# Broadcast rows fetched by DMA from a DRAM scratch in place of TensorE broadcasts, in a two-block transformer kernel

## The chip, the cores and the metric

The kernel runs on one core of a Trainium2 chip. The metric is the device time of one execution in microseconds (us). The five engines are called PE (TensorE matmul; PEld is its weight load), DVE (VectorE), ACT (ScalarE), POOL (GpSimd) and SP (SyncE, which here only issues DMAs).

## What is computed

Two blocks over 256 tokens of 1024 features, with 256 context tokens beside them, all in float32. The change is in the first block, a layer with a gated delta rule. Cut to what matters (forward direction; the backward one is the same on flipped tokens):

```python
proj = jnp.einsum('bld,dp->blp', hn, w_in)            # q,k,v | a,b | z_dn | u_pool | z_pool
qkv = jax.nn.silu(_short_conv(qkv, conv_w))
q, k = _l2_norm(q), _l2_norm(k)                       # every row to unit length
g = -jnp.exp(a_log) * jax.nn.softplus(ab[0] + dt_bias)
beta = jax.nn.sigmoid(ab[1])
# _gated_delta_rule, in chunks of 128 tokens: G = running sum of g in the chunk,
# decay factors exp(-|G_i - G_j|) between tokens, exp(G_i) on the queries
state = state * exp(G_last) + einsum('bhcd,bhcv->bhdv', k_i, v_new)
```

Behind it stand the output product, three feed-forward layers, a short-convolution mixer, a latent attention and a last feed-forward layer; the change leaves them as they are.

## The kernel before

**Layout.** Activations lie with features on the 128 partitions and the 512 tokens along the row. Every weight chunk (128 x 1024 values, eight 128 x 128 tiles) is loaded by SP into a ring of three `w_raw` buffers (L413), split by ACT into a high part `w_hi` (L777) and by POOL into a low part `w_lo` (L524), and used by PE in three products for each tile (L549, L550, L553). ACT splits chunk c+2 once chunk c-1 is done (`split_ahead`, `AHEAD = 2`).

**Order.** Each engine runs one hand-written instruction list in order; semaphores join them. In the input stage the chunks of `w_in` pass one after another: gates, keys, values, queries, then 26 tail items (`IN_TAIL`), here called n = 0 to 25. A "u" item is one of eight pooling inputs, which DVE turns into a pooled difference (`pooled_difference`); a "z" item gets a SiLU on ACT; items 13 and 25 are the pooling products themselves. ACT can write `u_hi(4)` only when item 13 is done on PE, for it reuses a buffer that item 13 reads.

**Unit lengths.** ACT takes square roots of the inverse squared lengths into `rk` (32 x 128) and `rq` (16 x 128) at n = 4 (`unit_length`, L999, L1000). The length of a token must then reach all partitions. PE does that with a one-hot stationary operand (`spread_lengths`, L894): four matmuls for each of 12 parts j (eight key heads, four pairs of query heads), placed behind the tail items n = 10, 11, 13, 14, 16, 17, 19, 20, 21, 22, 23 and 24, into bank 7 or 6, and DVE multiplies `kT` or `qT` by that bank (`scaled_by_length`, L1152).

**Running sums.** At n = 7 PE sums the gate terms and DVE copies them to `cum` (L1134 to L1139, semaphore `cum_ready`).

**The recurrence.** Eight rounds r = 0 to 7, each with a forward (FWD) and a backward (BWD) batch of four heads. `sums` (L1306) puts the running sums of a batch on all partitions, four matmuls with a broadcast gate column. `decay` on ACT turns them into `dec` = exp(-|G_i - G_j|) (four Abs at L1544, one Exp at L1548). `gram` (L1315) makes the keys' products, `masked_gram` on DVE (L1335) masks them, and `first_blocks` (DVE L1706 to L1717) starts the triangular inverse, whose matmuls are `left` (L1379) and `right` (L1390). Between two rounds PE does, for FWD and then BWD: `gram(r+1)`, `sums(r+1)`, `new_values(r)` (L1413). In rounds 4 to 7 the queries' factor exp(G) is made by ACT at the end of the round before, from the same bank as `sums` (`query_decay`, L1555), POOL multiplies it by the queries (L1682), and `out_four` (L1528, L1530) reads it. `dec` shares its room with `atl`, which `left` reads at its levels 3 and 4, and with the normalised inputs of the input stage. In between, PE works off 96 parts of the conditioning product (`mod_part`, L593), whose data SP streams through a ring of six buffers (L434).

## Time and profile before

| | |
|---|---|
| time, median of 3 runs (lowest to highest) | 2383.66 us (2382.59 to 2388.62) |
| the profiled execution: its time, its span | 2388.25 us, 2386.5 us |
| busy share of the span: PE, DVE, ACT, POOL | 96%, 38%, 33%, 43% |
| granted TensorE clock, mean | 0.981 of full |
| DMA: data moved, mean rate | 297.41 MB, 125 GB/s |

The span runs from 0 to 2386.5 us. The tail items of the input stage fill it up to about 289 us, the recurrence stands from there to about 560 us, and nothing behind that is edited. A busy engine is not necessarily the bound: the chain of waits and the timeline say which engine the next one waited for. In a timeline a bracket after a row is the idle time before it and what ended it.

### The profile page before, as it was taken

How to read it: one execution, taken by the hardware profiler on the slowest of the kernel's cores; microseconds unless marked ns; L12 is line 12 of the kernel's file. 1: busy time of each engine (PE TensorE's matmuls, PEld its weight loads, DVE VectorE, ACT ScalarE, POOL GpSimd, SP SyncE). 2: the span in 40 equal slices, each digit the busy share in tenths (PEclk: the TensorE clock that was granted, in tenths of full speed). 3: DMA queues.
4: the chain of work that ended last, by engine and by line, in shares of the span. 5: the costliest groups of instructions: out<-in, count | busy, mean ns of one | idle time of the engine just before them, and what ended most of it. 6: DMA issues, size and time to landing. Idle time of an engine off the chain costs nothing.

```text
span 2386.5 us, 37010 instructions
## 1 busy us (share of the span) xinstructions
PE 2280.5 (96%) x14398; PEld 1821.1 (76%) x14398; DVE 910.1 (38%) x1572; ACT 782.9 (33%) x1232; POOL 1024.2 (43%) x473
## 2 busy tenths in 40 slices
PE   6999999998979999999999999999999999898999
PEld 2788877776768888878877888887888887547999
DVE  4466456655551221153372131133121124756312
ACT  2445443332232222222223223224222223424444
POOL 0446522423524444434443444443444443204888
PEclk9999999999989999999999999999999999989999
DMA  7234455545625233224323423232432322203655
GB/s 253 89 101 138 151 204 187 187 150 197 223 69 170 95 97 95 90 79 150 121 92 113 142 90 98 90 96 80 168 96 91 97 94 71 71 0 91 192 184 185
DMA packets 82682, 297.41 MB, mean 125 GB/s; under 512 B 9072, under 2 KB 11504, under 8 KB 82288
## 3 DMA queue, kind: packets, MB, share of 16 engines
q1 hardware_dynamic: 82400, 295.06, 37.7%
q8 instruction: 108, 1.77, 0.3%
q10 hardware_dynamic: 144, 0.34, 0.1%
q14 instruction: 30, 0.25, 0.0%
HBM read 294.31 MB, written 1.05 MB: 124 GB/s over the span
## 4 chain that ended last, share of the span: by engine, by line
issue 57%; POOL 21%; PE 18%; DVE 2%; POOLq 1%; ACT 0%; DVEq 0%; ACTq 0%
POOL w_lo L524 21%; PE bank L549 3%; PE bank L550 3%; PE bank L553 3%; PE bank L593 2%; PE bank L1379 1%; PE bank L1390 1%; PE bank L1315 1%; PE bank L894 1%; PE bank L1362 0%; DVE gdn_outer L1727 0%; PE bank L1402 0%; PE bank L1306 0%; PE bank L1413 0%; POOLq L529 0%
## 5 line engine op out<-in xcount | busy, mean ns | idle before, releaser
L524 POOL TENSOR_TENSOR w_lo<-w_raw,w_hi 128x1024 fp32r<-128x1024 f32 x383 | 931.9, 2437 | 1159.8 <-ACT w_hi L777 1159.0
L549 PE MATMUL bank<-n_hi,w_lo 128*128 128x512 f32 (+1 forms) x2216 | 792.4, 358 | 18.0 <-ACT n_hi L748 9.3
L553 PE MATMUL bank<-n_lo,w_hi 128*128 128x512 f32 (+1 forms) x2216 | 786.2, 355 | 0.6 <-DVE n_lo L701 0.3
L550 PE MATMUL bank<-n_hi,w_hi 128*128 128x512 f32 (+1 forms) x2216 | 786.3, 355 | 0.0
L777 ACT CAST w_hi<-w_raw 128x1024 fp32r<-128x1024 f32 x383 | 401.5, 1050 | 770.5 <-PE bank L553 760.3
L549 PEld LDWEIGHTS bank<-n_hi,w_lo 128*128 128x128 f32 x2216 | 420.5, 190 | 95.4 <-issue 27.9
L553 PEld LDWEIGHTS bank<-n_lo,w_hi 128*128 128x128 f32 x2216 | 420.3, 190 | 67.0 <-DVE n_lo L701 2.5
L550 PEld LDWEIGHTS bank<-n_hi,w_hi 128*128 128x128 f32 x2216 | 420.7, 190 | 63.8
L2101 DVE TENSOR_TENSOR prod<-silu,bank 128x512 f32<-128x512 f32 (+1 forms) x88 | 54.6, 622 | 723.2 <-PE bank L553 723.1
L549 PE MATMUL bank<-g_hi,w_lo 128*128 128x512 f32 (+1 forms) x768 | 283.1, 369 | 1.4 <-DVE g_lo L2092 1.4
L550 PE MATMUL bank<-g_hi,w_hi 128*128 128x512 f32 (+1 forms) x768 | 283.1, 369 | 0.0
L553 PE MATMUL bank<-g_lo,w_hi 128*128 128x512 f32 (+1 forms) x768 | 283.0, 369 | 0.0
L2063 DVE SCALAR_TENSOR_TENSOR h<-bank,gates,h 128x256 f32<-128x256 f32 x136 | 60.7, 480 | 298.3 <-PE bank L553 298.1
L549 PEld LDWEIGHTS bank<-g_hi,w_lo 128*128 128x128 f32 x768 | 144.0, 188 | 28.8 <-DVE g_lo L2092 1.8
L553 PEld LDWEIGHTS bank<-g_lo,w_hi 128*128 128x128 f32 x768 | 144.0, 188 | 27.3
L550 PEld LDWEIGHTS bank<-g_hi,w_hi 128*128 128x128 f32 x768 | 144.0, 188 | 27.2
L2049 ACT ACTIVATE silu<-bank 128x512 f32<-128x512 f32 (+1 forms) x88 | 47.8, 544 | 284.9 <-PE bank L553 284.8
L1083 DVE SCALAR_TENSOR_TENSOR conv<-bank,cols,conv 128x508 f32<-128x508 f32 (+3 forms) x96 | 63.0, 659 | 58.8 <-ACT conv L1024 56.3
L2092 DVE TENSOR_TENSOR g_lo<-prod,g_hi 128x512 fp32r<-128x512 f32 (+1 forms) x88 | 84.6, 963 | 1.7 <-ACT g_hi L2039 1.5
L757 DVE TENSOR_TENSOR nt<-h 128x512 f32<-128x512 f32 (+1 forms) x77 | 79.1, 1028 | 2.6
L1661 POOL TENSOR_TENSOR gdn_t<-gdn_inner,consts 128x256 f32<-128x256 f32 x16 | 13.1, 817 | 155.3 <-DVE gdn_inner L1709 155.3
L593 PE MATMUL bank<-mod_raw,cond 128*32 128x512 f32 x256 | 60.1, 661 | 18.3 <-DMA mod_raw<-in_modstream 18.3
(320 smaller groups left out, 1964.6 us busy)
## 6 DMA issues: line engine op xcount, KB each, us to landing
w_raw<-in_stream SPq DMA_DIRECT2D x383, 512.0 KB, 3.5
mod_raw<-in_modstream SPq DMA_DIRECT2D x64, 512.0 KB, 5.6
late<-in_modstream SPq DMA_DIRECT2D x56, 512.0 KB, 4.6
w_raw<-in_modstream SPq DMA_DIRECT2D x48, 512.0 KB, 5.7
h<-in_tokens SPq DMA_DIRECT2D x1, 2048.0 KB, 11.6
consts<-in_consts SPq DMA_DIRECT2D x1, 1152.0 KB, 9.6
h<-in_ctx SPq DMA_DIRECT2D x1, 1024.0 KB, 8.8
out<-h SPq DMA_DIRECT2D x8, 128.0 KB, 3.6
```

The costliest lines, as they stand in the source:

```text
L524: nc.gpsimd.tensor_tensor(w_lo[:, slot, :], w_raw[:, slot, :], w_hi[:, slot, :].bitcast(F32), ALU.subtract).then_inc(w_lo_ready, 1)
L549: nc.tensor.matmul(out_ap, wl, hi, start=start, stop=False)
L550: nc.tensor.matmul(out_ap, wh, hi, start=False, stop=False)
L553: return nc.tensor.matmul(out_ap, wh, lo, start=False, stop=stop)
L593: last = nc.tensor.matmul(bank[MOD_BANK][32 * j:32 * j + 32, :], cond[:, which, k, :], room[:, jj * 512:(jj + 1) * 512], start=(k == 0), s ...
L757: square = nc.vector.tensor_tensor(nt[:, k % 2, s_], h[:, k, s_], h[:, k, s_], ALU.mult)
L777: nc.scalar.copy(w_hi[:, c % RING, :], w_raw[:, c % RING, :]).then_inc(w_hi_ready, 1)
L1083: ins = nc.vector.scalar_tensor_tensor(acc[:, :, to], src[:, :, of], col(Cols.CONV + ci * CONV + j), acc[:, :, to], ALU.mult, ALU.add)
L2049: nc.scalar.activation(silu[:, f % 2, 0:w], bank[(g0 + g) % BANKS][:, 0:w], ACT.Silu).then_inc(gate_ready, 1)
L2063: last = nc.vector.scalar_tensor_tensor(h[:, d, s_], bank[g % BANKS][:, s_], gates[:, gate, d, c:c + 1], h[:, d, s_], ALU.mult, ALU.add)
L2092: nc.vector.tensor_tensor(g_lo[:, f, 0:w], prod[:, f % 2, 0:w], g_hi[:, f, 0:w].bitcast(F32), ALU.subtract).then_inc(hid_lo, 1)
L2101: nc.vector.tensor_tensor(prod[:, f % 2, 0:w], silu[:, f % 2, 0:w], bank[g % BANKS][:, 0:w], ALU.mult).then_inc(groups_read, 2)
```

## The change

- `spread_lengths` is gone. ACT stores `rk` and `rq` to a DRAM scratch (`length_rows`) right after the square roots, and later loads each part back to all 128 partitions with a DMA whose source repeats one 2 KB row 128 times (`load_lengths`). The loads go into four rooms of `conv` and `act_out` that the convolutions have left. They are issued from ACT behind n = 7 (parts 0 to 3), 12 (4, 5), 15 (6, 7), 18 (8, 9) and 21 (10, 11). DVE multiplies from there.
- `sums` is gone. PE transposes `cum` once behind n = 10 (`turn_sums`), ACT copies it out and stores it behind n = 12 (`keep_sums`), and every batch's rows are loaded into `dec` itself (`load_decay`), two DMAs in front of round 0 and then two for each round, behind ACT's copies of level 4.
- The queries' factor gets a DMA of its own (`load_query_decay`, in rounds 4 to 7) and is made in its own round, between ACT's copies of level 2 and of `at`.
- PE's waits for `a_dec` and `a_qd` ahead of `key_rows` and ahead of the transposes of `a` are gone, since bank `b0` holds no sums any more. Some semaphores that nothing used are removed.

```diff
+    cum_rows = nc.dram_tensor("cum_rows", (64 * P,), F32).ap()
+    length_rows = nc.dram_tensor("length_rows", (6 * HEADS * P,), F32).ap()
+    def to_all(rows, first):
+        return bass.AP(rows.tensor, first * P, [[0, P], [1, 4 * P]])
...
+    KQ_LOADS = {7: (0, 1, 2, 3), 12: (4, 5), 15: (6, 7), 18: (8, 9), 21: (10, 11)}
+    def length_room(j):
+        return (conv, act_out)[j % 4 // 2][:, j % 2, :]
+    def turn_sums(pe):
+        pe.wait_ge(cum_ready, 1)
+        nc.tensor.transpose(bank[MISC_BANK][0:64, 0:P], cum[:].rearrange("p t g -> p (t g)"), C(Const.IDENT))\
+            .then_inc(gb_turned, 1)
...
-            for j in KQ_AFTER.get(n, ()):
-                spread_lengths(pe, j)
+            if n == 10:
+                turn_sums(pe)
...
-            nc.scalar.activation(rk[:], rk[:], ACT.Sqrt)
+            nc.scalar.activation(rk[:], rk[:], ACT.Sqrt).then_inc(kq_rstd, 1)
             nc.scalar.activation(rq[:], rq[:], ACT.Sqrt).then_inc(kq_rstd, 1)
+            act.wait_ge(kq_rstd, 2)
+            act.dma_start(length_rows[0:4 * HEADS * P].rearrange("(r c) -> r c", c=P), rk[:]).then_inc(rows_out, 16)
+            act.dma_start(length_rows[4 * HEADS * P:].rearrange("(r c) -> r c", c=P), rq[:]).then_inc(rows_out, 16)
+        def load_lengths(j):
+            if j == 0:
+                act.wait_ge(rows_out, 32)
+                act.wait_ge(tile_used, 24)
+            if j >= 4:
+                act.wait_ge(kq_scaled, j - 3)
+            act.dma_start(length_room(j), to_all(length_rows, 4 * j)).then_inc(length_full[j % 4], 16)
+        def keep_sums():
+            act.wait_ge(gb_turned, 2)
+            nc.scalar.copy(gb[:, 0:P], bank[MISC_BANK][0:64, 0:P]).then_inc(ab_act, 1)
+            act.wait_ge(ab_act, 5)
+            act.dma_start(cum_rows.rearrange("(r c) -> r c", c=P), gb[:, 0:P]).then_inc(rows_out, 16)
...
-            nc.vector.tensor_tensor(dest, dest, bank[kq_bank(j)][:], ALU.mult).then_inc(kq_scaled, 1)
+            nc.vector.tensor_tensor(dest, dest, length_room(j), ALU.mult).then_inc(kq_scaled, 1)
...
-                    sums(pe, r + 1, d)
...
-            act.wait_ge(g_cb, n + 1)
-            if r:
-                act.wait_ge(g_p1, nth(6, r - 1, 3, d))
+            act.wait_ge(rows_in[d], 16 * (r + 1))
             for j in range(4):
-                last = nc.scalar.activation(w["dec"][:, j], b4(b0)[:, j], ACT.Abs,
+                last = nc.scalar.activation(w["dec"][:, j], w["dec"][:, j], ACT.Abs,
...
+        act.wait_ge(rows_out, 48)
+        for d in (FWD, BWD):
+            load_decay(0, d)
         for d in (FWD, BWD):
             decay(0, d)
...
             tail_copy(r, 1, FWD)
+            if with_x:
+                load_query_decay(r)
...
+            if with_x:
+                query_decay(r)
             for n, d, t, hs, b0, gc in batches:
                 act.wait_ge(g_at, n + 1)
...
                     tail_copy(r, li, d)
+                    if li == 4 and r + 1 < len(ROUNDS):
+                        load_decay(r + 1, d)
```

## Rows read from the trace of the kernel before

**Rows 1.** Windows: stretch, length, busy us (count) of each engine, granted clock, DMA share, GB/s

```profile
263.00:274.00 11.00, 11.00 (x88) 10.37 (x88) 4.77 (x8) 4.15 (x7) 7.19 (x4) 1.00 0.48 143
357.00:389.00 32.00, 30.77 (x511) 23.40 (x511) 20.88 (x50) 12.86 (x35) 8.17 (x8) 1.00 0.55 197
```

**Rows 2.** Chain of work that ended last, the length broadcasts: start, us, what

```profile
229.90 1.08 PE bank L894 x8
233.97 1.08 PE bank L894 x8
240.90 1.08 PE bank L894 x8
...
283.28 1.08 PE bank L894 x8
```

**Rows 3.** Timeline of ACT in the input stage: start, us, instruction, [idle before]

```profile
212.28 0.29 ACT L1000 ACTIVATE rq<-rq 16x128 f32<-16x128 f32 x1
...
221.62 1.05 ACT L777 CAST w_hi<-w_raw 128x1024 fp32r<-128x1024 f32 x1
...
241.01 0.40 ACT L994 CAST u_hi<-boxr 128x256 fp32r<-128x256 f32 x1 [5.68 <-PE bank L553]
```

**Rows 4.** Timeline of POOL in the input stage

```profile
242.71 7.17 POOL L524 TENSOR_TENSOR w_lo<-w_raw,w_hi 128x1024 fp32r<-128x1024 f32 x3 [4.90 <-ACT w_hi L777]
```

**Rows 5.** Timeline of DVE in the input stage

```profile
228.79 0.23 DVE L1139 TENSOR_TENSOR e_tail<-tot,cum 128x64 f32<-128x64 f32 x1
```

**Rows 6.** Timeline of PE: three idle times

```profile
204.31 0.60 PE L860 MATMUL bank<-decay_rate,consts 16*128 16x16 f32 x2 [3.50 <-DVE decay_rate L1117]
...
224.05 0.35 PE L549 MATMUL bank<-n_hi,w_lo 128*128 128x256 f32 x1 [1.39 <-POOL w_lo L524]
...
461.56 0.46 PE L1528 MATMUL bank<-gdn_qdec,state 128*128 128x128 f32 x2 [1.77 <-DVE gdn_rhs L1761]
```

**Rows 7.** Windows, behind the first of these idle times

```profile
206.00:208.00 2.00, 2.00 (x12) 2.00 (x11) 0.00 (x0) 0.00 (x0) 2.00 (x1) 0.50 0.51 199
```

**Rows 8.** DMA issues: line, queue, count, KB each, median us to landing; one ACT issue

```profile
mod_raw<-in_modstream SPq DMA_DIRECT2D x64, 512.0 KB, 5.6
rope<-in_rope ACTq DMA_DIRECT2D x1, 331.0 KB, 3.1
...
L2352 ACTq DMA_DIRECT2D rope<-in_rope x1: 379/379/379, 2024.0 to 2024.0; - x1
```

**Rows 9.** Chain of work that ended last, from round 1 to round 2

```profile
353.29 0.89 PE bank L1306 x8
...
355.08 0.91 PE bank L1315 x8
358.69 0.96 DVE gdn_inner L1712
359.70 0.68 PE bank L1379 x16
```

**Rows 10.** Timeline of DVE and of PE, from round 6 to round 7

```profile
539.99 0.95 DVE L1712 TENSOR_TENSOR gdn_inner<-gdn_inner,consts 128x256 f32<-128x256 f32 x1
...
545.12 0.68 PE L1379 MATMUL bank<-gdn_outer,gdn_inner 64*64 64x64 f32 x16
```

**Rows 11.** Timeline of ACT: a level-4 copy of round 1; `decay` of round 0, FWD

```profile
341.09 0.37 ACT L1560 COPY gdn_t<-bank 128x256 f32<-128x256 f32 x1 [1.52 <-PE bank L1379]
...
289.42 1.14 ACT L1544 ACTIVATE gdn_dec<-bank,neg_cum 128x128 f32<-128x128 f32 x4 [4.78 <-PE bank L553]
...
291.87 0.63 ACT L1548 ACTIVATE gdn_dec<-gdn_dec 128x512 f32<-128x512 f32 x1
```

**Rows 12.** Waits of SP in the recurrence: us in total, times, longest us

```profile
SPq L434 <- PE bank L593: 205.3, 37, 18.3
```

**Rows 13.** DVE's square of two SBUF inputs: beside an idle POOL; the mean of all (page, costliest groups)

```profile
15.00 0.69 DVE L757 TENSOR_TENSOR nt<-h 128x512 f32<-128x512 f32 x1
...
L757 DVE TENSOR_TENSOR nt<-h 128x512 f32<-128x512 f32 (+1 forms) x77 | 79.1, 1028 | 2.6
```

68 lines of the change are left out of this document (22 added, 46 removed).

## The prediction, made before the changed kernel ran

> **What bounds the kernel now.** I read the windows by stage first. Look at PE's busy time against the length of the stretch: in the tail of the input stage it is busy 11.00 of 11.00 us, in a round of the recurrence 30.77 of 32, both at full clock [rows 1]. So PE time taken out there shows in the end time, until another engine's chain becomes the longer one. The chain of waits then says which PE work stands on the path: all 12 length broadcasts do [rows 2], and so does the FWD broadcast of sums between two rounds [rows 9]. The timelines of ACT, POOL and DVE say how soon another engine takes over. Behind the recurrence everything hangs on its end (SP loads the next chunks only then), so what is saved ahead of it is saved in the whole.
>
> **Input stage, what is removed.** From one broadcast to the next it is 4.07 us with one chunk between them and 6.93 with two [rows 2]. So a chunk takes 2.86 and a broadcast 1.21 us, twelve of them 14.5. The transpose that comes in is one matmul of the four in a broadcast: 0.3.
>
> **Input stage, what ACT takes on.** A DMA issue holds ACT for 0.38 us; between issue and landing a 331 KB load took 3.1 us and the 512 KB loads of the modulation stream 5.6 [rows 8]. The new ones carry 256 KB. I walk through the items with these numbers.
>
> At n = 4 two issues and the wait for the roots put about 0.9 us behind 212.28 [rows 3]. The next pooling input starts that much later, and the chain runs through DVE, ACT and POOL to the idle time of 1.39 us in which PE waits for `w_lo` at 224.05 [rows 6]; PE passes the 0.9 us on in full. At n = 7 four issues (1.5 us, of which the running SiLU hides 0.3) stand ahead of the cast at 221.62 [rows 3] and of the fourth pooling input. So `cum_ready`, at 229.0 [rows 5], comes at 229.0 + 0.9 + 1.2 = 231.1. Item 10 ends at 229.9 + 0.9 = 230.8, the transpose waits until 231.1, and item 11 starts at 231.5, where it started at 229.90 + 1.08 = 231.0. So far 0.5 us is lost.
>
> Items 11, 12 and 13 then take 3 x 2.86, and item 13 ends at 240.1 (before: 240.9 [rows 2]). Here is the next obstacle. ACT may write `u_hi(4)` only now (241.01, after 5.68 us idle [rows 3]); behind it stand the SiLU and the cast of chunk 15, and POOL works from 242.71, 7.17 us for three chunks [rows 4]. The low part of chunk 15 was therefore ready at 245.1, 4.2 us after item 13. Two broadcasts and chunk 14 covered this with 5.3 us; now chunk 14 alone covers 2.86. In addition `keep_sums` stands ahead of that cast (copy and wait, about 0.4 us) with three issues (1.15): ready at 240.1 + 4.2 + 1.5 = 245.8. PE idles 2.8 us and starts chunk 15 at 245.8, before 240.9 + 2 x 1.21 + 2.86 = 246.2. The gain up to here is 0.4 us, and four broadcasts have gone.
>
> From there seven more broadcasts (j = 4 to 10) go until 283.28, and PE is the bound: a chunk's cast (1.05 [rows 3]) and low part (2.4) with SiLU and two issues are done 5.1 us after the chunk that frees them, where PE needs them after 2 x 2.86 = 5.7. That is 7 x 1.21 = 8.5. The loads at n = 15, 18 and 21 wait for products that DVE makes only behind a pooled difference; three times 0 to 0.5 us, I take 0.5 in all. Item 24 ends 0.4 + 8.5 - 0.5 = 8.4 us earlier. Bounds: 13.0 if ACT's issues cost PE nothing and nothing stalls (11 x 1.21 - 0.3); 3 if each wait costs a microsecond more and the clock falls once.
>
> DVE's product now reads two SBUF tiles beside a working POOL. A square of two such inputs takes 0.69 us alone and 1.03 in the mean [rows 13]. For two products per part pair that is 0.7 us, in DVE time that is idle, so I cost it at nothing; if the cover is gone, it is in the 0.5 above. The Trainium skill ("SBUF — State Buffer", section "Who interferes with whom") says that a DVE instruction with two SBUF inputs and a GpSimd instruction that reads SBUF exclude each other for whole instructions. By that rule a product could wait for a whole low part; the gain would then be some 3 us less.
>
> **First round.** The twelfth broadcast began at 283.28 and the FWD Exp of `decay` ended at 292.50, 9.2 us later, with 3.1 us from its first Abs on [rows 2, 11]. Now ACT issues the two loads about 0.8 us after item 24. SP has just sent the context tokens and three modulation parts, so I take 3.5 us to landing (bounds 2.5 and 6). `dec` is there 0.8 + 3.5 + 3.1 = 7.4 us after item 24, 1.8 earlier; with a little for the second issue I take 1.5 (bounds: a landing in 3.1 us gives 2.2, one in 5.6 a loss of 0.3). The page "DMA: Bandwidth & Descriptors" of the Trainium skill (section on the anatomy of one DMA) gives about 2 us plus the bytes at 436 GB/s, an estimate of 2.6 us here, by which this term would be 2.4.
>
> **Between the rounds.** The chain runs `gram` FWD, `sums` FWD (0.89), `new_values` FWD, `gram` BWD (355.08), then DVE until 359.65, and `left` at 359.70 [rows 9]. Without `sums` FWD, `gram` BWD ends 0.89 us earlier, and DVE, which waits for it, too. `sums` BWD stands beside DVE's chain and is worth nothing. In front of round 7, DVE is done at 540.94 and `left` starts at 545.12 [rows 10]: PE itself is the bound there, and both broadcasts count, 1.78. Together 6 x 0.89 + 1.78 = 7.1 us (bounds: 6.2 if DVE holds the last one too, 8.9 if PE itself bounds two more).
>
> **What hides the new work of the rounds.** `load_decay` is issued behind the level-4 copy at 341.09 [rows 11]. `first_blocks` wants `dec` once `gram` BWD (then over at 355.1) is masked (0.7), and `decay` takes 1.8 (3.1 less the 1.3 of a table load between its Abs and its Exp [rows 11]); so the rows must be there by 354, 12 us after their issue, against 3.1 to 5.6. The issues (0.38) stand in waits for PE such as the 1.52 us there. The queries' two Exp (0.63 each) fall into ACT's wait for the transposes of `a`; with that cover gone they cost 1.3 us in each of four rounds. SP waited 205.3 us for PE in the recurrence [rows 12], so DMA time is to be had for 0.5 to 1 MB more a round. PE no longer waits for `a_dec` and `a_qd`, and it did not before.
>
> **Sum.** 8.4 + 1.5 + 7.1 = 17.0 us. The profiled execution took 2388.25 us (a span of 2386.5), so 2371.2 of its own kind. The median of the runs, 2383.66, is 4.6 us lower: 2366.7.
>
> **Rivals.**
> *Nothing takes over from PE.* If ACT's sequencer issues the DMAs beside its running work and the cast of chunk 15 is in time, it is 13.0 + 2.2 + 8.9 = 24 us: 2360. For it: ACT is busy 4.15 of 11 us [rows 1]. Against it: its idle time is waiting for PE, and the issues come behind that wait. Chance 0.2.
> *The clock falls.* After idle times of 1.39 and 1.77 us PE stays at 2.4 GHz; after 3.50 it runs on at a granted clock of 0.50, 1.2 GHz [rows 6, 7]. The change makes idle times of 2.8 at chunk 15, of 2.3 at 224 and of about 2.7 (1.77 + 2 x 0.89 - 0.89) in front of rounds 5 and 6, all between. Each fall costs about one chunk's time, 2.9 us; three of them leave 8 us: 2375. Chance 0.17.
> *The input stage gives nothing.* The chain of ACT, DVE and POOL is longer than walked, and only the rounds gain, 6 us: 2378, no change that could be told. Chance 0.1.
> *Slower: the rows land late.* All 128 reads of a load go to one 2 KB row of DRAM, which no row shows. The first load costs its whole delay; the seven later ones have 12 us. At a landing time of L the loss against my sum is (L - 3.5) + 7 x (L - 12): 17.0 us at L = 13.1, from where the kernel is slower, and 24.2 (0.3% slower) at 14.0; at 20 us it would be 72.5, or 2439. Against it: that is over four times the 3.1 of the ACT queue's own load [rows 8]. Chance 0.05.
>
> **Numbers.** My forecast has a chance of 0.48, and the time is its own: 2366.7 us. The range of 2356 to 2379 takes in the full gain, with 4 us for ends that I did not walk, the fallen clock and most of the empty input stage, and leaves out the late rows. A change of 0.3% (7.2 us) is about what a measurement of this kernel can tell. The forecast, the full gain and the fallen clock are faster by more; the empty input stage is not: 0.83 faster, 0.12 the same, 0.05 slower.
>
> **What the profile after would show.** No L894 and L1306; chunks of 2.86 us in a row behind item 16; an idle time of nearly 3 us in front of chunk 15 ended by POOL's `w_lo`; the transpose of the sums ended by `cum_ready` near 231; ACT's loads landing in 2.5 to 6 us; `decay` right behind the `xt` copies, long before `gram`; 0.9 us less from `gram` FWD to `left` in each round; PE idle near 2.7 us in front of rounds 5 and 6. The prediction is wrong if the granted clock drops there, if POOL or DVE passes grow beside each other, or if ACT waits for `rows_in` between the rounds.

## The result, and the profile after

The changed kernel takes 2398.49 us, the median of 5 runs (2397.05 to 2400.23), where the kernel before takes 2383.66 in the same session (5 runs too, 2382.59 to 2388.62). The ratio is 1.0049, with a 95% interval of 1.0037 to 1.0061. So it is slower by 0.5%, where 0.7% faster was forecast. The profiled execution took 2397.05 us, with a span of 2394.7, 8.2 us more than before. Line numbers are 4 to 6 higher than before up to the start of the input stage, and 1 to 14 higher from there on.

Where did the forecast 17 us go, and where do the 8 come from? I read the same event in both traces, place by place. The difference (after less before) grows or shrinks only where something is lost or won:

| event | before, us | after, us | difference |
|---|---|---|---|
| last SiLU of the pooling gate (item 24) | 283.32 | 278.92 | -4.4 |
| first `left` of round 0 | 295.63 | 296.30 | +0.7 |
| first `left` of round 7 | 545.12 | 540.52 | -4.6 |
| SP's first load behind the recurrence | 577.45 | 575.35 | -2.1 |
| root in front of the second FFN | 1246.23 | 1243.67 | -2.6 |
| root in front of the third FFN | 1628.23 | 1626.97 | -1.3 |
| root in front of the attention | 2008.59 | 2013.46 | +4.9 |
| root in front of the last FFN | 2189.51 | 2195.69 | +6.2 |
| first store of the output | 2378.24 | 2385.71 | +7.5 |

The change is over at 575, and the kernel is then 2.1 us ahead. 10.1 us are lost behind 1246, where not a line was changed. Three losses ahead of that ate most of the gain. The rows of each follow.

**Input stage.** Windows: stretch, length, busy us (count) of PE, PEld, DVE, ACT and POOL, granted clock, DMA share, GB/s. The first answers to the first of [rows 1], the second to the second.

```profile
263.00:274.00 11.00, 10.02 (x86) 9.85 (x85) 7.55 (x9) 5.71 (x10) 8.21 (x4) 1.00 0.75 244
357.00:389.00 32.00, 29.89 (x504) 22.24 (x500) 21.77 (x53) 13.12 (x35) 8.35 (x9) 1.00 0.61 218
```

PE was busy in all of the 11 us before, and now it is idle for one of them. The DMA share went from 0.48 to 0.75. The timeline of PE (start, us, instruction, idle time before it and what ended it) shows the forecast transpose, the forecast idle time in front of chunk 15 (3.65 us, forecast 2.8), and four that the forecast has not or has smaller:

```profile
217.73 0.36 PE L555 MATMUL bank<-n_hi,w_lo 128*128 128x256 f32 x1 [2.02 <-POOL w_lo L530]
225.67 0.36 PE L555 MATMUL bank<-n_hi,w_lo 128*128 128x256 f32 x1 [1.43 <-POOL w_lo L530]
...
231.40 0.27 PE L889 MATMUL bank<-consts,cum 128*64 128x128 f32 x1
...
246.57 0.36 PE L555 MATMUL bank<-n_hi,w_lo 128*128 128x256 f32 x1 [3.65 <-POOL w_lo L530]
...
266.14 0.36 PE L555 MATMUL bank<-n_hi,w_lo 128*128 128x256 f32 x1 [0.98 <-POOL w_lo L530]
...
275.84 0.36 PE L555 MATMUL bank<-n_hi,w_lo 128*128 128x256 f32 x1 [0.98 <-POOL w_lo L530]
```

The timelines of POOL and of DVE show what stands in front of the last one. Three low parts in a row took 7.17 us before [rows 4], and a pair of DVE's products 1.3:

```profile
253.69 7.20 POOL L530 TENSOR_TENSOR w_lo<-w_raw,w_hi 128x1024 fp32r<-128x1024 f32 x3 [2.13 <-ACT w_hi L783]
263.62 7.55 POOL L530 TENSOR_TENSOR w_lo<-w_raw,w_hi 128x1024 fp32r<-128x1024 f32 x3 [2.73 <-ACT w_hi L783]
273.31 7.98 POOL L530 TENSOR_TENSOR w_lo<-w_raw,w_hi 128x1024 fp32r<-128x1024 f32 x3 [2.14 <-ACT w_hi L783]
```

```profile
268.09 3.63 DVE L1166 TENSOR_TENSOR kT<-kT,act_out 128x512 f32<-128x512 f32 x2
271.98 1.28 DVE L1166 TENSOR_TENSOR qT<-qT,conv 128x512 f32<-128x512 f32 x2
274.09 4.96 DVE L1166 TENSOR_TENSOR qT<-qT,act_out 128x512 f32<-128x512 f32 x2 [0.83 <-DMA act_out<-length_rows]
```

The pair at 271.98 ran while POOL was idle and took 1.28 us. The pair at 274.09 lies across POOL's three low parts and took 4.96, and POOL took 7.98 where it had taken 7.20. That is the rule of the Trainium skill which the prediction weighed ("SBUF — State Buffer", section "Who interferes with whom"), and the trace agrees with it: a product waits for a whole low part (2.4 us) or holds one up.

The clock fell behind the idle time in front of chunk 15: from 247.6 to 250.8 us the granted clock is 0.50, where it is 1.00 in the kernel before (245 to 250). In return it is 0.50 only from 206.8 to 210 behind the idle time of 3.5 us near 205, where before it is 0.50 from 203.6 to 210.2. The mean from 190 to 285 is 0.96 in both.

**First round.** The timeline of ACT, and DVE's first instruction of the round:

```profile
278.92 0.38 ACT L1057 ACTIVATE y_pool<-bank 128x256 f32<-128x256 f32 x1 [2.52 <-PE bank L559]
279.46 1.05 ACT L783 CAST w_hi<-w_raw 128x1024 fp32r<-128x1024 f32 x1 [0.16 <-DMA w_raw<-in_stream]
282.81 1.07 ACTq L1539 DMA_DIRECT2D gdn_dec<-cum_rows  x2
289.95 1.28 ACT L1546 ACTIVATE gdn_dec<-gdn_dec,neg_cum 128x128 f32<-128x128 f32 x4 [9.44 <-DMA gdn_dec<-cum_rows]
```

```profile
293.27 0.85 DVE L1720 TENSOR_TENSOR gdn_inner<-gdn_a,gdn_dec 64x256 f32<-64x256 f32 x2 [8.82 <-ACT gdn_dec L1550]
```

The loads were to be issued 0.8 us behind item 24 and went out 3.9 us behind it: in ACT's program they stand behind the wait for the last four pooling groups. They landed 7.1 us later (289.95), behind 1 MB of context and three loads of modulation weights that SP had sent at 279.2 to 282.8. I had taken 3.5 us. The prediction's sentence on the Trainium skill ("DMA: Bandwidth & Descriptors", section on the anatomy of one DMA) has an estimate of 2.6 us. The section is on DMAs issued by GpSimd; of the 16 loads of `load_decay`, issued by ACT, the shortest took 3.0 us.

The rows are not all of this loss. PE stood first for the modulation weights, for which it had not waited before:

```profile
292.14 2.80 PE L599 MATMUL bank<-mod_raw,cond 128*32 128x512 f32 x8 [8.50 <-DMA mod_raw<-in_modstream]
296.30 0.68 PE L1383 MATMUL bank<-gdn_outer,gdn_inner 64*64 64x64 f32 x16 [1.35 <-DVE gdn_inner L1726]
```

These matmuls are over at 294.94, and the wait for the rows adds 1.35 us. So with earlier rows alone `left` would have started near 295 in this trace, 0.7 us ahead of before and not 4.4. Both loads have to come earlier.

**Last round.** Here the profile shows a wait for which the prediction put no price. ACT, then PE, in round 7:

```profile
541.26 0.81 ACTq L1557 DMA_DIRECT2D gdn_qdec<-cum_rows  x2
...
546.45 0.37 ACT L1567 COPY gdn_t<-bank 128x256 f32<-128x256 f32 x1 [0.45 <-PE bank L1383]
548.96 0.63 ACT L1562 ACTIVATE gdn_qdec<-gdn_qdec 128x512 f32<-128x512 f32 x1 [2.14 <-DMA gdn_qdec<-cum_rows]
550.93 0.63 ACT L1562 ACTIVATE gdn_qdec<-gdn_qdec 128x512 f32<-128x512 f32 x1 [1.34 <-DMA gdn_qdec<-cum_rows]
551.46 1.05 ACT L1600 COPY gdn_at<-bank 128x512 f32<-128x512 f32 x2
```

```profile
552.08 2.05 PE L1453 MATMUL bank<-qT,kT 128*128 128x128 f32 x16 [2.43 <-ACT gdn_at L1600]
```

ACT stands for the query rows, and behind it stand the copies of the turned `a`, for which PE waits 2.43 us. The DMA issues (count, KB each, median us to landing) show the landing times; [rows 8] had 3.1 and 5.6:

```profile
gdn_dec<-cum_rows ACTq DMA_DIRECT2D x16, 256.0 KB, 3.5
gdn_qdec<-cum_rows ACTq DMA_DIRECT2D x8, 256.0 KB, 8.7
conv<-length_rows ACTq DMA_DIRECT2D x6, 256.0 KB, 4.8
act_out<-length_rows ACTq DMA_DIRECT2D x6, 256.0 KB, 5.2
```

**Behind 1246.** The two halves of an FFN are one loop in PE's program (`with pe.Fori(0, 2)` in `pe_ffn`). These are PE's rows where the second half of the second FFN begins, and of the third:

```profile
1433.92 0.39 PE L559 MATMUL bank<-g_lo,w_hi 128*128 128x512 f32 x1
1434.33 0.47 PE L555 MATMUL bank<-n_hi,w_lo 128*128 128x512 f32 x1
1437.34 0.39 PE L556 MATMUL bank<-n_hi,w_hi 128*128 128x512 f32 x1 [2.54 <-issue]
...
1820.23 0.50 PE L555 MATMUL bank<-n_hi,w_lo 128*128 128x512 f32 x1 [3.41 <-issue]
```

"issue" says that PE waited for nothing that the profile knows: no semaphore, no engine, no DMA. In the kernel before, the same place runs through:

```profile
1438.12 0.40 PE L553 MATMUL bank<-g_lo,w_hi 128*128 128x512 f32 x1
1438.35 0.39 PE L549 MATMUL bank<-n_hi,w_lo 128*128 128x512 f32 x1
1438.59 0.40 PE L550 MATMUL bank<-n_hi,w_hi 128*128 128x512 f32 x1
```

What is left to look at is the fetching of the program itself. The DMA queues on the page of the profile have one of kind "instruction": 116 packets with 1.90 MB, 16 KB each (before: 108 packets, 1.77 MB). The page "Runtime: NRT & Kernel Launch" of the Trainium skill (section on instruction fetch mechanics) says that an engine's program is fetched in blocks of 16 KiB, 256 instructions, and that a taken branch to a place that is not held waits for a fetch. The change takes 455 instructions out of PE's program in front of these loops (counted in the built programs, with a weight load and a matmul for each pass: 48 matmuls of lengths, 64 of sums, and waits). Modulo 256 the starts of the four loops move from 237, 133, 137 and 46 to 38, 190, 194 and 103. Whether that is the cause was the first thing to test.

### The profile page after: what moved, and what is told of

Its sections match the earlier page's. It is cut to its first block, busy times and chain, and to the rows that moved or that the text cites. A ratio compares the mean times of both kernels' runs of the same rounds, so it can differ in the third digit from the quotient of the medians.

```text
span 2394.7 us, 36582 instructions
## 1 busy us (share of the span) xinstructions
PE 2257.5 (94%) x14175; PEld 1798.0 (75%) x14175; DVE 919.0 (38%) x1572; ACT 785.0 (33%) x1233; POOL 1025.4 (43%) x473
## 4 chain that ended last, share of the span: by engine, by line
issue 60%; POOL 24%; PE 11%; DVE 2%; POOLq 1%; DMA 1%; ACT 1%; DVEq 0%; ACTq 0%
POOL w_lo L530 24%; PE bank L599 2%; PE bank L555 1%; PE bank L559 1%; PE bank L556 1%; PE bank L1383 1%; PE bank L1394 1%; PE bank L1323 1%; DVE gdn_outer L1741 0%; DMA gdn_qdec<-cum_rows 0%; PE bank L1406 0%; PE bank L1366 0%; POOLq L535 0%; DMA gdn_dec<-cum_rows 0%; POOLq L529 0%
## 5 line engine op out<-in xcount | busy, mean ns | idle before, releaser
L555 PE MATMUL bank<-n_hi,w_lo 128*128 128x512 f32 (+1 forms) x2216 | 792.9, 358 | 28.7 <-POOL w_lo L530 11.6
## 6 DMA issues: line engine op xcount, KB each, us to landing
h<-in_tokens SPq DMA_DIRECT2D x1, 2048.0 KB, 10.1
```

Source lines behind the costliest of these rows:

```text
L555: nc.tensor.matmul(out_ap, wl, hi, start=start, stop=False)
```

## Experiments

Each was timed in 5 rounds beside the kernel before on the same chip. Ratios are to that kernel; where they come from different chips they compare to 1 or 2 us only. Drifts are read as in the table above. The medians of the kernel before were 2388.3 us beside a_shift24, b_shift57, b_shift40 and len_only, 2388.2 beside a_same, sums_only, a_qlate and a_early, 2389.0 beside a_sp24, len_sp20, a_all24 and a_all60, and 2387.3 beside b_shift80 and the two of one bank.

### Where the code lies

**a_shift24.**

```
             for q in range(MOD_PARTS):
+                if q == 3:
+                    for _ in range(24):
+                        pe.wait_ge(cond_ready, 1)
                 mod_part(pe, q)
```

> The kernel after, with 24 further instructions in TensorE's program (48 waits for a semaphore that is long up, two to an instruction, put where TensorE waits for the fourth part of the modulation weights anyway, 9.3 to 15.1 us). They move all later code of TensorE by 24 instructions and change no work. Theory A (where the code lies): the program of TensorE is fetched in blocks of 16 KB = 256 instructions; the change takes 455 instructions out ahead of the four loops over FFN halves, so that the jumps back of the second and third loop land 4 instructions or fewer in front of a block's end, and TensorE stands for the next block (2.54 us at 1437.34, 3.41 us at 1820.23). 24 instructions further the jumps land behind that border: both idle times go, and with them the lower clock behind them; 2388 to 2392 us. Theory B (the time is lost by the change's transfers or by chance of one execution): nothing changes, 2397 to 2400 us, and the two idle times stay.

The kernel that ran has 24 waits, so 12 further instructions and not the 24 of the expectation: its trace holds 36594 instructions, that of the kernel after 36582. The four loops start at 50, 202, 206 and 115. a_sp24 and a_all24, which name this run as their base, do have 24 further instructions (62, 214, 218, 127).

Measured: 2390.07 us, ratio 1.0009 (1.0000 to 1.0018), where the kernel after had 1.0049. Both idle times are gone: 12 instructions are enough. From 1244 to 2188 us this kernel and the kernel before run alike (it is 2.0 us ahead at 1244.25, 1.9 at 2187.59). In the fourth loop PE stands:

```profile
2288.41 0.36 PE L555 MATMUL bank<-n_hi,w_lo 128*128 128x256 f32 x1 [1.86 <-issue]
```

**b_shift57** (the same edit of the kernel before, with 114 waits).

> The kernel before, unchanged in its work, with 57 further instructions in TensorE's program at the same early place, so that the four loops over FFN halves lie exactly as in the kernel after, counted modulo 256 instructions (38, 190, 194, 103). Theory A: the kernel before gets the idle times of the kernel after, about 2.5 and 3.4 us with issue as their end at the second half of the second and third loop, and takes 2390 to 2394 us. Theory B: 2383 to 2385 us and no such idle time.

Measured: 2401.77 us, ratio 1.0062 (1.0050 to 1.0075), 13.5 us slower than the kernel before. That is more than the 2390 to 2394 us that were expected; the span of the trace is 11.2 us longer. Up to 1246 its trace is that of the kernel before (1246.45 for 1246.23), then it loses 3.7 us in the second FFN, 5.0 in the third and 1.2 from there to the first store:

```profile
1436.93 0.39 PE L549 MATMUL bank<-n_hi,w_lo 128*128 128x512 f32 x1
1440.91 0.40 PE L550 MATMUL bank<-n_hi,w_hi 128*128 128x512 f32 x1 [3.59 <-issue]
...
1825.78 0.50 PE L549 MATMUL bank<-n_hi,w_lo 128*128 128x512 f32 x1 [3.30 <-issue]
```

The idle times came to the kernel before at the same instructions. No work differs.

**b_shift40** (80 waits).

> As the run with 57, with 40 further instructions: the second and third loop start 17 instructions earlier in the block (173 and 177, so some 20 instructions in front of its end). Theory A: TensorE has about 10 matmuls of 0.23 us more to work on while the next block comes, so the idle times shrink by about 2 us each, to 0 to 1.5 us; 2384 to 2387 us. Theory B: as before, 2383 to 2385 us, no idle time with issue as its end.

Measured: 2397.01 us, ratio 1.0040 (1.0024 to 1.0056). The idle times are as forecast, the total is not:

```profile
1438.82 0.39 PE L553 MATMUL bank<-n_lo,w_hi 128*128 128x512 f32 x1
1440.45 0.50 PE L549 MATMUL bank<-n_hi,w_lo 128*128 128x512 f32 x1 [1.24 <-issue]
...
1822.14 0.39 PE L550 MATMUL bank<-n_hi,w_hi 128*128 128x512 f32 x1 [1.69 <-issue]
...
2293.95 0.36 PE L549 MATMUL bank<-n_hi,w_lo 128*128 128x256 f32 x1 [3.17 <-issue]
```

The second half of the second FFN began at 1436.95, so PE worked for 2.3 us before it stood for 1.24: together 3.5, where it stood for 3.59 behind a single matmul with 57. The fourth loop (start at 86) lost 3.17, which I had not forecast: of the 7.2 us that this trace is behind at its first store, 5.1 come in the last FFN.

**b_shift80** (160 waits; it tells the position from the number of added waits).

> The kernel before with 80 further instructions of TensorE; the four loops start at 61, 213, 217 and 126 of a block. Theory A: no idle time with issue at its end in the second and third loop, 1.9 us in the fourth, and 2 to 3 us at the start for the waits (57 brought 1.6 us there): 2 to 5 us slower than before and 8 to 11 us faster than with 57. Rival (the added waits cost by their number): slower than with 57, 18 us over before.

Measured: 2392.22 us, ratio 1.0021 (1.0012 to 1.0030): with more waits, 9.6 us less than with 57. The second and third FFN show no such idle time (1627.83 and 2008.17, before 1628.23 and 2008.59); the fourth loop shows 2.05 us at 2290.07. So the number of waits is not what decides.

**a_same** (199 instructions, 100 at the place above and 99 in front of the output stage).

> The kernel after with 199 further instructions in TensorE's program (waits for semaphores that are long up: 100 in front of the fourth part of the modulation weights, 99 in front of the output stage's first matmul, both where TensorE stands for 5 us anyway), so that the four loops over FFN halves lie exactly as in the kernel before, modulo 256 (237, 133, 137, 46). Its difference to the kernel before is the change without its shift of the code. Theory A with the stage times of the shift by 24 (2.6 us ahead at the end of the recurrence, kept to the last stage, where the loop at 127 lost 1.9 us that the one at 46 does not): no idle time with issue as its end at a loop's second half, 1.5 to 3 us faster than before. Rival (the last stage's 1.9 us are no matter of the position): within 1 us of before.

Measured: 2399.54 us, ratio 1.0046 (1.0033 to 1.0059). The forecast was wrong. No idle time with issue as its end is left at any of the four loops, but I had put the waits where PE "stands for 5 us anyway", and 99 of them are not hidden by that:

```profile
592.75 0.55 PE L555 MATMUL bank<-n_hi,w_lo 128*128 128x256 f32 x1 [10.31 <-issue]
```

In the kernel before it is 5.47 us there, ended by DVE. An instruction that only waits for what is long there takes PE's sequencer about 0.1 us (10.31 us for 99), and the first 100 put the first root 2 to 3 us back (40.21; 37.5 before). The run says nothing on the net worth of the change, but it is the base for a_qlate and a_early, which carry the same waits.

**The jumps themselves.** The traces hold the jump back of each loop as an instruction of PE's sequencer. This is the one of the fourth loop, in the kernel after and in the kernel before (duration in ns, three times the same number, and start in us):

```profile
L2029 PEldq COMPARE_BRANCH  x1: 3362/3362/3362, 2292.7 to 2292.7; - x1
...
L2015 PEldq COMPARE_BRANCH  x1: 223/223/223, 2286.5 to 2286.5; - x1
```

The 17 traces of this document have 68 such jumps, four in each. Every one takes either 0.21 to 0.25 us or 3.3 to 5.0 us, and in all four loops the start of the loop, modulo 256 by the count above, tells which. Starts at 202 to 254 and at 21 to 64 have the short jump, starts at 74 to 194 the long one, without an exception. The packets of the instruction queue agree: there are 98 to 100 in the traces with one long jump, 107 or 108 with two, 116 or 118 with three. So it seems that behind a long jump the loop's program is fetched again. That agrees with what the Trainium skill ("Runtime: NRT & Kernel Launch", section on instruction fetch mechanics) says of a taken branch to a place that is not held.

Whether PE's matmuls notice depends on what they have queued. In the second and third loop (0.23 us for a matmul) the long jumps from 133 and 137 cost nothing: in the kernel before they take 3.37 and 3.36 us, and PE runs through. Only the starts just in front of the border (173 to 194) have an idle time there, and it falls some instructions behind the start. In the fourth loop (0.12 us for a matmul) every long jump is followed by an idle time 1.7 to 1.8 us shorter than the jump: 1.62 behind 3.36, 1.86 behind 3.62, 3.17 behind 4.96, twelve traces in all.

### The parts of the change

**len_only** (the kernel before with the lengths' part of the diff alone, and 20 instructions).

> Only the lengths go by DMA; the running sums are spread by TensorE as before. 20 further instructions in TensorE's program keep the four loops away from the end of a block (64, 216, 220, 129). Theory 1 (the input stage gave 4.3 us in the trace after, because VectorE's products of two SBUF operands hold up GpSimd's low halves: threes of 7.5 us in place of 7.17, and pairs of up to 4.96 us in place of 1.3): the input stage ends 3 to 5 us earlier than before, the rest keeps it: 2379 to 2382 us. Theory 2 (the input stage was worth what was forecast and lost it at its end to the first round's loads): 2374 to 2377 us.

Measured: 2384.56 us, ratio 0.9987 (0.9977 to 0.9997), 3 us faster; the last pooling SiLU starts at 278.43 (-4.9), the first `left` at 293.02 (-2.6). Theory 1 held.

**sums_only** (the kernel after with the lengths spread by PE as before, and 6 instructions).

> Only the running sums go by DMA; the lengths are spread by TensorE as before (the second one item later, behind the sums' turn in its bank). 6 further instructions bring the four loops to the positions of before (237, 133, 137, 46). By the stage times: the input stage as before or up to 1 us later, the first round 3 to 5 us later than there (its rows are loaded at its end), rounds 1 to 6 gain 5 to 6 us, the last gives 4 back: 1 to 4 us slower than before. Rival (the sums' part gains what was forecast and only the lengths' part fails): 5 to 8 us faster than before.

Measured: 2392.23 us, ratio 1.0013 (1.0004 to 1.0022), 3 us slower. The first `left` starts at 300.08 (+4.5), that of round 7 at 545.67 (+0.6), SP's first load behind the recurrence at 583.73 (+6.3). The sums' part alone is a loss: the rounds between win 3.9 us, the first and the last give back more.

**a_qlate.**

```
-            if with_x:
-                query_decay(r)
             for n, d, t, hs, b0, gc in batches:
                 act.wait_ge(g_at, n + 1)
...
                     if li == 4 and r + 1 < len(ROUNDS):
                         load_decay(r + 1, d)
+            if with_x:
+                query_decay(r)
```

> As a_same, and in the rounds with queries ScalarE takes the exponent of the queries' rows behind the copies of levels 3 and 4, no longer in front of the copies of the turned matrices. Theory C (the new wait is the loss at the end of the recurrence: the query rows land 7.7 us after their issue, ScalarE stands in front of its copies of the turned matrices until then, TensorE 2.4 us for these copies and 1.4 us longer in the matmuls behind): the last round takes 4.0 us less, the round before 1.0 to 1.5 us less, in all 4 to 6 us faster than a_same. Rival (the matmuls behind are bound elsewhere, by GpSimd's product with the query decay, which now comes later): 0 to 1 us.

Measured: 2391.74 us, ratio 1.0014 against 1.0046 of a_same, 7.8 us less at the medians, more than the 4 to 6 expected. The traces are 4.7 us apart at SP's first load behind the recurrence. From the first `left` of round 7 to SP's first load it is 32.32 us, where it is 36.43 in a_same, 36.27 in a_shift24, 34.83 in the kernel after and 32.33 in the kernel before. Theory C held for the last round. ACT and PE, to set beside those of the kernel after:

```profile
551.74 1.07 ACT L1601 COPY gdn_at<-bank 128x512 f32<-128x512 f32 x2 [1.36 <-PE bank L1450]
...
558.11 1.15 ACT L1565 ACTIVATE gdn_qdec<-gdn_qdec 128x512 f32<-128x512 f32 x2
```

```profile
553.14 2.05 PE L1456 MATMUL bank<-qT,kT 128*128 128x128 f32 x16
```

The same wait costs 2.5 us in the trace after and 4.1 in a_same. A part of such differences is the clock: the matmuls behind it took 2.05 us in the kernel after, at a granted clock of 1.00 (552 to 555), and 3.49 in a_shift24, where the wait is 2.43 us too but the clock is 0.50 (550 to 553).

**a_early** (the loads of the first round's rows, issued earlier into two free rooms).

```
+                if n == 23:
+                    act.wait_ge(rows_out, 48)
+                    act.wait_ge(kq_scaled, 10)
+                    for n_, d, t, hs, b0, gc in per_batch(0):
+                        act.dma_start(conv[:, d, :], to_all(cum_rows, 16 * t + gc.start)).then_inc(rows_in[d], 16)
...
-        act.wait_ge(rows_out, 48)
-        for d in (FWD, BWD):
-            load_decay(0, d)
...
+                rows = w["dec"][:, j] if r else conv[:, d, j * P:(j + 1) * P]
```

> As a_same, and the rows of the first round come to two rooms of the lengths while the last chunks of the input stage are worked on (issued at the sixth-last chunk's place, read from there by the first round's distances), in place of a load behind the wait for the last pool group. Theory D (the first round is held by its rows: issued at 282.8, landed at 290, and VectorE waits 8.8 us for the decay): VectorE's first blocks begin near 286, but TensorE still stands for the modulation weights that land at 292, which lie in front of its first left product: the first left product moves from 296 to 294 or 295, 1 to 2 us faster than a_same. Rival (the rows are no limit, the modulation weights are all of it): within 0.5 us of a_same.

Measured: 2393.05 us, ratio 1.0023, 6.5 us less than a_same at the medians and 5.5 by the ratios. The first `left` starts at 293.41, where it starts at 299.61 in a_same. I had expected 1 to 2 us, since PE waits for the modulation weights too. But in a_same their matmuls are over at 295.4, and PE stands 4.17 us more for the rows; in a_early it goes from them to the first `left` at once.

**a_sp24** (SP's order of loads).

```
-        sp.wait_ge(normed, KT)
-        sp.dma_start(h[:, :, L:T], ctx2[:]).then_inc(ctx2_in, 16)
...
             if r == 3:
+                sp.wait_ge(normed, KT)
+                sp.dma_start(h[:, :, L:T], ctx2[:]).then_inc(ctx2_in, 16)
                 sp.wait_ge(w_lo_ready, IN_LOADS)
```

> As a_shift24, and SyncE sends the three loads of modulation weights for the first round ahead of the context's 1 MB, not behind it. Theory E (the first round waits for both: the decay rows and the modulation weights land late because the context's 10.8 us lie in the same 16 engines): both land 2 to 4 us earlier, the first left product moves by as much, and the kernel is 2 to 4 us faster than a_shift24. Rival (the rows of the first round are the limit, and they land late by their own issue at 282.8): within 1 us of a_shift24.

Measured: 2390.34 us, ratio 1.0009, the same as a_shift24 (which has 12 instructions fewer, so the two differ in more than SP's order). The rival held: the weights' matmuls are over at 289.0, and PE then waits for the rows.

```profile
298.01 1.12 PE L1386 MATMUL bank<-gdn_outer,gdn_inner 64*64 64x64 f32 x16 [9.03 <-DVE gdn_inner L1729]
```

**len_sp20.**

> As len_only (lengths by DMA, sums by TensorE, 20 further instructions), and the context's load behind the three loads of modulation weights. In len_only the first left product starts at 293.02 behind the wait for modulation weights; with them early it starts at 288 to 290, and the kernel is 3 to 4 us faster than len_only, 6 to 8 us faster than before. Rival (the sums and the decay of the first round are ready no earlier): within 1.5 us of len_only.

Measured: 2383.58 us, ratio 0.9981 (0.9972 to 0.9990). The trace shows what was forecast (first `left` at 288.52), and its span of 2379.4 is 7.1 us under that of before; the timed runs give 4.5 us, and 1.4 us against len_only. That is between theory and rival, and not settled.

### What the lengths' loads and products cost the input stage

**one_bank.**

```
                 turn_sums(pe)
+                pe.wait_ge(kq_rstd, 2)
+                for t in range(4):
+                    last = nc.tensor.matmul(bank[MOD_BANK][:, t * P:(t + 1) * P],
+                                            C(Const.IDENT, 4 * HEADS)[:, t:t + 1].to_broadcast([4 * HEADS, P]), rk[:],
+                                            start=True, stop=True)
+                last.then_inc(kq_bc, 1)
...
-            nc.vector.tensor_tensor(dest, dest, length_room(j), ALU.mult).then_inc(kq_scaled, 1)
+            dve.wait_ge(kq_bc, 1)
+            nc.vector.tensor_tensor(dest, dest, bank[MOD_BANK][:], ALU.mult).then_inc(kq_scaled, 1)
```

> As a_shift24 (20 in place of 24 further instructions and five others), but all twelve products of VectorE take their second operand from one PSUM bank, in which TensorE spreads the key lengths of the first head once; the twelve loads of lengths are issued and waited for as before. It scales all heads by the lengths of the first head. Theory F (VectorE's products of two SBUF operands and GpSimd's low halves hold each other up): each product takes 0.68 us, no pair over 1.4 us, GpSimd's threes of low halves 7.2 us in place of 7.5 to 8.0, and the input stage ends 1 to 3 us earlier than in a_shift24 less the 1.2 us of the one broadcast: 0 to 2 us faster than a_shift24. Rival (the input stage is bound by the casts, the weights' DMA and GpSimd, not by the products): 0.5 to 1.5 us slower than a_shift24, for the broadcast.

**one_bank_nold.**

```
-                for j in KQ_LOADS.get(n, ()):
-                    load_lengths(j)
...
-            dve.wait_ge(length_full[j % 4], 16 * (j // 4 + 1))
```

> As one_bank, and the twelve loads of lengths are left out (ScalarE does not issue them, their 3 MB do not move); the two stores stay. Scaled by the first head's lengths as there. Theory G (the loads cost the input stage time, by 0.36 us of ScalarE each and by the DMA share of 0.60 in place of 0.47, so that the weights land late for the casts): 1 to 3 us faster than one_bank. Rival (hidden): within 1 us of one_bank.

Both kernels scale every head by the lengths of the first head. Measured: 2390.81 and 2388.03 us, ratios 1.0011 (1.0000 to 1.0021) and 1.0001 (0.9990 to 1.0013). The runs time the first against a_shift24 (1.0009) as no change. In the traces the products are back at 0.68 us. The groups of POOL's low parts and of DVE's products in the input stage (busy us, mean ns) show it; first the kernel after, then one_bank:

```profile
L530 POOL TENSOR_TENSOR w_lo<-w_raw,w_hi 128x1024 fp32r<-128x1024 f32 x26 | 63.6, 2456 | 31.4 <-ACT w_hi L783 31.2
L1166 DVE TENSOR_TENSOR kT<-kT,act_out 128x512 f32<-128x512 f32 x4 | 8.5, 2173 | 0.0
```

```profile
L530 POOL TENSOR_TENSOR w_lo<-w_raw,w_hi 128x1024 fp32r<-128x1024 f32 x26 | 62.2, 2402 | 31.2 <-ACT w_hi L783 31.0
L1177 DVE TENSOR_TENSOR kT<-kT,bank 128x512 f32<-128x512 f32 x8 | 5.1, 679 | 0.0
```

From the first root to the last pooling SiLU (the start of a run differs by 1 to 2 us from one execution to the next) it is 245.8 us before, 240.7 after, 241.1 in a_shift24, 239.8 in one_bank and 237.2 in one_bank_nold. The last two hold one broadcast of 1.2 us that the change has not. By these five traces the products cost 2.5 us (241.1 - 239.8 + 1.2) and the loads 2.6 (239.8 - 237.2); without both and without that broadcast the input stage would have gained 9.8. But the same stretch is 240.7 to 243.7 us in five traces whose input stage is the same (the kernel after, a_shift24, a_sp24, a_same, a_qlate), so neither share stands clear of that scatter; the two together do. PE's idle time in the stretch from 195 us scatters less. Summed over idle times above 0.3 us it is 12.1 to 13.6 us in the kernel after (12.6) and the seven runs made from it that keep loads and products, 10.5 in one_bank and 8.6 in one_bank_nold. That gives very roughly 2 us to each. The timed runs show 2.8 us between the medians for the loads and nothing for the products.

### A faster version

**a_all24** has the edits of a_qlate, a_early and a_sp24 together.

> As a_shift24, with three edits together: the query exponents behind the copies of levels 3 and 4 (4.1 us in the last round by a_qlate), the first round's rows loaded early (5.5 us by a_early against a_same), the context's load behind the three loads of modulation weights. If the mended waits are all that stood between the change and its gain, the first left product comes at 286 to 290, the recurrence ends 12 to 16 us ahead of before, and the kernel takes 12 to 15 us less than a_shift24, 10 to 14 us less than before. Rival (each mend uncovers the same next wait, the input stage's last casts): 6 to 9 us less than a_shift24.

Measured: 2376.88 us, ratio 0.9960 (0.9946 to 0.9975): 12 us faster than the kernel before at the medians and 9.6 by the ratio, and further ahead of the kernel after. The expectation (10 to 14 us) held. The first `left` starts at 289.74 (-5.9), and SP's first load at 565.81 (-11.6). In the first round ACT still waits for its rows, now for 3.16 us:

```profile
283.39 1.28 ACT L1555 ACTIVATE gdn_dec<-conv,neg_cum 128x128 f32<-128x128 f32 x4 [3.16 <-DMA conv<-cum_rows]
```

**a_all60.**

> As a_all24 with 60 in place of 24 further instructions: the four loops start at 98, 250, 254 and 163 of a block. It asks for the fourth loop alone, whose jump back cost 1.9 us at 103 and at 127, 3.2 us at 86 and nothing at 46. By theory A the second and third loop lie behind the border and show nothing. For the fourth no rule is at hand; if it goes by the distance of the jump's target to the border (near 196), 33 instructions in front of it cost more than 69: 2.5 to 3.6 us idle there. The time at the start grows by 3 us or less for the 36 further waits. 1 to 4 us slower than a_all24.

Measured: 2383.88 us, ratio 0.9986 (0.9976 to 0.9996), 6 to 7 us slower than a_all24, where 1 to 4 were expected. The trace has no idle time in the second and third loop, and 1.70 and 2.19 us in the fourth. Its span of 2377.7 is only 0.8 us longer than that of a_all24. The profiled execution (2379.72 us) is one of the fast ones of this kernel, whose runs lie between 2378.51 and 2391.45; what the slower ones lose is not in it.

## Why the prediction was wrong, point by point

The step that failed most is the sentence on what bounds the kernel: "Behind the recurrence everything hangs on its end, so what is saved ahead of it is saved in the whole." The work there hangs on that end; the time it takes does not stay the same. The change also shortens PE's program, and with it moves code that nobody edited. The kernel loses 10.1 us there in the trace (from -2.6 to +7.5). The three idle times make up 7.6 of them (2.54, 3.41 and 1.62). The rest goes with the clock, which is 0.50 near 1630, 1821 and 2020 us, where it is 1.00 in the kernel before; the fall near 2020 lies in the attention, and no run shows that the jumps bring it. That the position of the code is the cause is shown in both directions: 12 instructions put back take 9.5 us from the kernel after (1.0049 to 1.0009), and 57 put into the kernel before bring it 13.5 us and the same idle times at the same instructions.

But the position explains at most 10 of the 25 us between forecast and trace. The other terms, in the order of the sum:

| term | forecast | in the trace | what the runs showed |
|---|---|---|---|
| input stage | -8.4 | -4.4 | about 5 us for the loads and for DVE and POOL holding each other up; some 2 each by PE's idle time |
| first round | -1.5 | +5.1 | the rows go out 3.1 us later than I had it and take 7.1 us, not 3.5; the modulation weights hold PE to 294.94 |
| between the rounds | -7.1 | -5.3 | -6.0 over the first six; +0.7 in front of round 7, where -1.78 was forecast |
| queries' exponents, round 7 | 0 | +2.5 | the wait for their rows; gone in a_qlate |
| behind 1246 | 0 | +10.1 | the position of the code (b_shift57, a_shift24): 7.6 idle, the rest with the clock |

The first four give -2.1 us, and with 10.1 and what lies between the stages the trace ends at +8.2. At a better position of the code (a_shift24) the change is worth nothing that can be told from no change.

*Input stage.* The walk through the items held where it was detailed: the transpose at 231.40 (forecast 231.1), the idle time in front of chunk 15 until 246.57 (245.8). Two steps failed. "In DVE time that is idle, so I cost it at nothing" was wrong, because POOL pays for it as well. And of the loads only ACT's issues were counted, not their bytes, with a DMA share of 0.75 for 0.48. PE waits for low parts at 266.14 and 275.84; one_bank has one such wait (0.80 us at 272.38), one_bank_nold none. The sentence of the prediction on the rule of two SBUF inputs named "some 3 us less"; the trace has 4.0 less, about half of them from this.

*First round.* The mechanism (rows late at the end of the input stage) was seen, its size not. The later issue was readable before: ACT's 4.78 us for the last pooling groups stand in front of `decay` in [rows 11]. That SP's 1 MB of context was in flight was known too. The bound of 6 us to landing was too small. And the prediction did not ask when the modulation weights land: in the kernel before they were there when PE came to them (291.06), in the kernel after PE came at 283.6 and stood for them for 8.50 us.

*Between the rounds.* The mechanism held, and for six of seven its size: from `left` to `left` rounds 0 to 5 take 0.9 us less each (one 1.4), and PE is busy 29.89 us in the stretch that had 30.77 [rows 1], 0.88 less. Round 6 takes 0.7 us more; in a_qlate it takes 1.0 less (36.95 for 37.92), so that is the queries' wait as well.

*Queries.* "The queries' two Exp fall into ACT's wait for the transposes" costed the instructions and not the wait for their rows. These are issued 7 us ahead of their use (at 541.26, and the matmuls whose result is to be copied end at 548.58) and landed after 8.7 us at the median, where I had looked at 3.1 to 5.6 for other loads. The rival "the rows land late" was meant for `load_decay`, whose 12 us of cover were enough (3.5 us at the median, no wait of ACT for it but in the first round).

*The clock.* This rival came true in part. Behind the idle time at chunk 15 (3.65 us, listed with 2.8) the granted clock was 0.50 for 3 us; in the mean of the input stage the shorter fall near 205 made up for it. Behind those in front of rounds 5 and 6 (2.66 and 2.65 us, forecast 2.7) it stayed at 1.00 in the kernel after, but not in every trace: in a_sp24, behind 2.65 and 2.66 us at the same places, it is 0.50 (458.5 to 461.5 and 503 to 506), and `left` to `left` then takes 41.1 and 43.4 us, where the kernel after has 39.6 and 40.9. So one execution does not settle what such an idle time costs.

*The chances.* The three faster outcomes of the prediction (0.48, 0.20, 0.17) add up to 0.85, not to its 0.83.

*The fourth loop.* It lost nothing at 46 and 1.6 to 3.2 us at every start from 86 to 163, for there its jump is long. In five of these traces the profile puts the wait down to POOL's low part. In the kernel after that part was done at 2295.60, the jump at 2296.08, and PE's matmul began at 2296.51, so it was the jump.

What stays open: why a long jump takes 3.3 us once and 5.0 at another time, and why five of the twelve traces show a second idle time of 0.5 to 2.2 us some 4 us later. The mechanism is not shown either. The body of a loop is 1664 instructions, six and a half blocks of 256, and the two places where short and long starts meet (between 194 and 202, and between 64 and 74) are about half a block apart. A store for a fixed number of blocks, which holds the start for a body that ends in its seventh block and has dropped it for one that ends in its eighth, would give just that; this is an inference from the 68 jumps.

## What to carry to other kernels

This kernel, with loops of 1664 instructions on TensorE, gained or lost 0.4 to 0.6% when 12 to 57 instructions were added at one early place. So look at the stages that a change doesn't touch, at the duration of the jumps, and at idle times that end with "issue" right behind one, before judging a change; if they differ, compare the kernels at an equal position of the code. When TensorE work is moved to DMA, place the consumer's wait behind everything that others wait for, issue the load as early as its room is free, and count the bytes against the stream that is already running. Moving a product's operand from PSUM to SBUF had a price on GpSimd too: 7.98 us for three low parts in place of 7.20.

## What the runs showed of the hardware that I had not expected

- A jump back over 1664 instructions took TensorE's sequencer 0.21 to 0.25 us or 3.3 to 5.0, by the start of the loop modulo 256 alone (68 jumps in 17 traces).
- With a start just in front of the border (190 and 194) the second and third loop stood idle for 2.5 to 3.6 us; with 10 matmuls of 0.23 us between start and border (b_shift40) the idle time was 1.24.
- Each long jump goes with 8 to 10 further packets of 16 KB on the instruction queue (98 in a_shift24 with one, 107 in a_same with two, 116 in the kernel after with three).
- Waits that are long fulfilled are not free on TensorE's sequencer: 99 instructions with two each took 10.31 us.
- A load in which all 128 partitions read one 2 KB row of DRAM landed after 3.0 us at the least, 3.5 at the median between the rounds, and 8.7 beside the loads of modulation weights. Both kinds read one shared row, so that is not what makes the difference between them.
